# The opening of a one-layer hybrid decoder step: order of the first loads, of the first weight splits, and of the second weight tile's first token group

## What is computed

```python
def rmsnorm(x, g):
    xf = x.astype(jnp.float32)
    y = xf * lax.rsqrt(jnp.mean(xf * xf, axis=-1, keepdims=True) + EPS)
    return (y * g.astype(jnp.float32)).astype(x.dtype)
...
    xn = rmsnorm(h, norm_mix)
    z = xn @ w_in
    conv_out, new_a = causal_dwconv(z[..., O_C:O_H] * z[..., O_H:O_QKV], buf_a, conv_a_w)
    y_a = z[..., O_B:O_C] * conv_out
    qkv, new_qkv = causal_dwconv(z[..., O_QKV:O_G], buf_qkv, conv_qkv_w)
...
    g = -jnp.exp(a_log.astype(f32)) * jax.nn.softplus(z[..., O_A:O_BETA].astype(f32) + dt_bias.astype(f32))
    beta = jax.nn.sigmoid(z[..., O_BETA:IN_W].astype(f32))
```

## Time and profile before

| | us |
|---|---|
| runs of the kernel before, median (lowest to highest of 3) | 1250.08 (1249.86 to 1250.35) |
| the profiled execution, its own time | 1247.68 |
| its span | 1245.9 |
| TensorE busy | 1231.8 (99%) |
| VectorE busy | 789.4 (63%) |
| GpSimd busy | 647.4 (52%) |
| ScalarE busy | 455.5 (37%) |

### The profile page before, as it was taken

One profiled execution on the slowest core, in us unless ns is written; L12 is line 12 of the kernel. 1 busy time (PEld: TensorE's weight loads), 2 busy tenths in 40 slices (PEclk: granted clock), 3 DMA queues, 4 the chain that ended last, 5 costly groups with the idle time before them and its releaser, 6 DMA issues.

```text
span 1245.9 us, 20234 instructions
## 1 busy us (share of the span) xinstructions
PE 1231.8 (99%) x7854; PEld 1083.5 (87%) x7854; DVE 789.4 (63%) x1258; ACT 455.5 (37%) x790; POOL 647.4 (52%) x500
## 2 busy tenths in 40 slices
PE   7999999999999999999999999999999999999998
PEld 6899999899999999998878888888887888877886
DVE  6466899535554655645997686565566667556642
ACT  6465654421212212214333333333434533433412
POOL 2333110112112221214889898888789989787730
PEclk9999999999999999999999999999999999999999
DMA  6122672843223323231145344444655442542012
GB/s 206 45 80 71 173 206 77 216 140 94 78 76 105 92 69 87 78 91 50 48 165 172 124 158 139 140 144 153 227 170 203 166 139 102 187 128 92 18 56 85
DMA packets 163793, 151.05 MB, mean 121 GB/s; under 512 B 21079, under 2 KB 139251, under 8 KB 161010
## 3 DMA queue, kind: packets, MB, share of 16 engines
q1 hardware_dynamic: 140722, 136.88, 34.8%
q10 hardware_dynamic: 22976, 12.88, 3.8%
HBM read 103.25 MB, written 46.49 MB: 120 GB/s over the span
## 4 chain that ended last, share of the span: by engine, by line
PE 95%; issue 1%; DVE 1%; POOL 1%; DMA 1%; ACT 0%; SPq 0%; POOLq 0%; DVEq 0%; ACTq 0%
PE banks L2374 15%; PE banks L2376 15%; PE banks L2377 15%; PE banks L1808 12%; PE banks L1810 11%; PE banks L1809 11%; PE banks L2405 1%; PE banks L2391 1%; PE banks L2503 1%; PE banks L2502 1%; PE banks L2507 1%; PE banks L1994 1%; PE banks L2319 1%; DMA w_raw<-in_w_in 1%; PE banks L1987 1%
## 5 line engine op out<-in xcount | busy, mean ns | idle before, releaser
L1808 PE MATMUL banks<-xn_high,w_high 128*128 128x384 f32 (+1 forms) x672 | 226.9, 338 | 1.0 <-DVE xn_low L2586 0.9
L1810 PE MATMUL banks<-xn_high,w_low 128*128 128x384 f32 (+1 forms) x672 | 219.8, 327 | 0.0
L1809 PE MATMUL banks<-xn_low,w_high 128*128 128x384 f32 (+1 forms) x672 | 219.6, 327 | 0.0
L1027 POOL TENSOR_TENSOR w_low<-w_raw,w_high 128x1024 fp32r<-128x1024 f32 x30 | 77.9, 2598 | 231.2 <-ACT w_high L1297 231.2
L3362 DVE TENSOR_TENSOR hT<-hT,banks 128x512 f32<-128x512 f32 x148 | 98.3, 684 | 97.6 <-PE banks L2377 96.5
L1808 PEld LDWEIGHTS banks<-xn_high,w_high 128*128 128x128 f32 x672 | 127.8, 190 | 5.1 <-issue 1.2
L2374 PE MATMUL banks<-op_high,set_high 128*128 128x512 f32 x336 | 131.8, 392 | 0.0
L2376 PE MATMUL banks<-op_low,set_high 128*128 128x512 f32 x336 | 130.9, 390 | 0.0
L2377 PE MATMUL banks<-op_high,set_low 128*128 128x512 f32 x336 | 130.9, 389 | 0.0
L1809 PEld LDWEIGHTS banks<-xn_low,w_high 128*128 128x128 f32 x672 | 128.1, 191 | 0.0
L1810 PEld LDWEIGHTS banks<-xn_high,w_low 128*128 128x128 f32 x672 | 127.6, 190 | 0.0
(11 more groups left out here) (421 smaller groups left out, 2765.5 us busy)
## 6 DMA issues: line engine op xcount, KB each, us to landing
op_raw<-ops_kept SPq DMA_DIRECT2D x21, 1024.0 KB, 4.9
w_up_raw<-in_w_up SPq DMA_DIRECT2D x16, 1024.0 KB, 6.6
w_raw<-in_w_in SPq DMA_DIRECT2D x28, 512.0 KB, 4.6
ops_kept<-u_rows SPq DMA_DIRECT2D x28, 512.0 KB, 2.7
ops_kept<-u_T SPq DMA_DIRECT2D x42, 256.0 KB, 2.4
w_down_half<-in_w_down SPq DMA_DIRECT2D x3, 2048.0 KB, 9.5
w_down<-in_w_down SPq DMA_DIRECT2D x24, 256.0 KB, 4.0
w_raw<-in_w_out SPq DMA_DIRECT2D x8, 512.0 KB, 4.0
```

The costliest lines, as they stand in the source:

```text
L1027: pool.tensor_tensor(w_l[n % 2][:, :, :], w_raw[n % 2][:, :, :], w_h[n % 2][:, :, :].bitcast(F32), ALU.subtract).then_inc(w_low, 1)
L1808: pe.matmul(bank[:, 0:w], w_h[n % 2][:, k, :], hi[:, c0:c0 + w], start=(k == first), stop=False)
L1809: pe.matmul(bank[:, 0:w], w_h[n % 2][:, k, :], lo[:, c0:c0 + w], start=False, stop=False)
L1810: ins = pe.matmul(bank[:, 0:w], w_l[n % 2][:, k, :], hi[:, c0:c0 + w], start=False, stop=(k == last))
```

## The change

- x_small is loaded on ScalarE's queue behind c_main, ahead of the norm weights; SyncE's queue begins with x_big[0] and holds weight tiles 0 and 1 one behind the other, then x_big[3:5], ab_raw and x_big[5:8].
- The low part of weight tile 0 is made by GpSimd (after the power of token tile 3), that of weight tile 1 by VectorE (after scale_x(3)); the high part of weight tile 1 is made by ScalarE right after the eighth slice's.
- On TensorE, weight tile 0 with group 0 multiplies high weights slice by slice as the slices come, and the low weights from k = 5 on; then weight tile 1 with group 0 follows at once (it was step u = 3, behind the ab products), and the first ab product is made in two halves with turned slices between them.
- Idle products: 6, 2 and 1 of 104 columns ahead of token tiles 0, 1 and 2, where 3 of 208 stood ahead of tile 0.
- The ab products use banks 2, 6 and 7; slices of groups 1 and 2 are turned into four banks (4 to 7), four ahead, where they were five and five; the history rows go to banks 4 and 5.
- ScalarE's squares 4 and 5 follow the high part of weight tile 1, then the ab weights' high part, then square 6; GpSimd makes the ab weights' low part after the power of token tile 5.
- The products finish in another order, so waits on acc_done use in_done(n, g): tile 0's groups finish as 1, 3, 4 and tile 1's as 2, 5, 6. The parts left out of the diff below are this replacement of `3 * n + g + 1` or `3 * (n - 1)` at seven further waits.

```diff
@@ -394,6 +394,12 @@
 
+        def in_done(n, g):
+
+            if n < 2:
+                return ((1, 3, 4), (2, 5, 6))[n][g]
+            return 3 * n + g + 1
+
         def out_bank(n, g):
@@ -606,16 +612,17 @@
 
-        SQUARE_AFTER = {7: (4, 5, 6), 8: (7,), 10: (8,)}
+        SQUARE_AFTER = {7: (4, 5), 8: (7,), 10: (8,)}
         AB_AFTER = 9
-        IDLE_PRODUCTS = (3, 0, 0)
-        TURN_AHEAD = 5
+        IDLE_PRODUCTS = (6, 2, 1)
+        TURN_AHEAD = 4
+        AB_BANKS = (2, 6, 7)
         SEEDED = 1
 
         def turn_bank(g, k):
 
             m = KT * g + k
-            return k if g == 0 else 3 + (m - KT) % 5
+            return k if g == 0 else 4 + (m - KT) % 4
 
@@ -713,8 +720,6 @@
 
-            sp.dma_start(x_small[0:NS, :], xs_v).then_inc(s_xin[0], 16)
-            sp.dma_start(x_small[NS:C0, :], meta_tokens).then_inc(s_xin[0], 16)
             sp.dma_start(x_big[:, 0:1, :], xp_v[:, 0:1, :]).then_inc(s_xin[1], 16)
@@ -848,10 +853,12 @@
                     step(3 * (n - 3) + 1)
-                load(n)
+                if n != 1:
+                    load(n)
                 if n == 0:
+                    load(1)
+                    sp.dma_start(x_big[:, 3:5, :], xp_v[:, 3:5, :]).then_inc(s_xin[4], 16)
                     sp.dma_start(ab_raw[:, :, :], w_in_v[:, :, O_A:O_A + 8]).then_inc(s_ahead, 16)
-                    sp.dma_start(x_big[:, 3:5, :], xp_v[:, 3:5, :]).then_inc(s_xin[4], 16)
                     sp.dma_start(x_big[:, 5:8, :], xp_v[:, 5:8, :]).then_inc(s_xin[5], 16)
@@ -1023,13 +1030,15 @@
                 if n >= 2:
-                    pool.wait_ge(acc_done, 3 * (n - 1))
+                    pool.wait_ge(acc_done, in_done(n - 2, 2))
                 pool.tensor_tensor(w_l[n % 2][:, :, :], w_raw[n % 2][:, :, :], w_h[n % 2][:, :, :].bitcast(F32),
                                    ALU.subtract).then_inc(w_low, 1)
 
             for t in range(NT):
                 x_power(t)
                 if t == 3:
+                    split_low(0)
+                if t == 5:
                     pool.wait_ge(ab_hi, 1)
@@ -1127,7 +1136,7 @@
                     history_a(i)
-                if n not in LOW_BY_DVE:
+                if n and n not in LOW_BY_DVE:
                     split_low(n + 1)
@@ -1287,13 +1296,15 @@
             act.dma_start(cm[:, :], c_main[:, 0:2 * P + 2 * C0 + 2 * NH]).then_inc(s_const, 16)
+            act.dma_start(x_small[0:NS, :], xs_v).then_inc(s_xin[0], 16)
+            act.dma_start(x_small[NS:C0, :], meta_tokens).then_inc(s_xin[0], 16)
             act.dma_start(rows_n[0:8, :], norm_mix.rearrange("l (k p) -> (l k) p", p=P)).then_inc(s_norm, 16)
             act.dma_start(rows_n[8:16, :], norm_ffn.rearrange("l (k p) -> (l k) p", p=P)).then_inc(s_norm, 16)
             def split_high(n):
 
                 act.wait_ge(w_load[n % 2], 16 * (n // 2 + 1))
                 if n >= 2:
-                    act.wait_ge(acc_done, 3 * (n - 1))
+                    act.wait_ge(acc_done, in_done(n - 2, 2))
                 act.activation(w_h[n % 2][:, :, :], w_raw[n % 2][:, :, :], ACT.Copy).then_inc(w_high, 1)
@@ -1308,7 +1319,7 @@
                 act.wait_ge(ab_made, g + 1)
-                act.activation(abT[:, c0:c0 + w], ps[7 - g % 2][0:16, 0:w], ACT.Copy).then_inc(ab_kept, 1)
+                act.activation(abT[:, c0:c0 + w], ps[AB_BANKS[g]][0:16, 0:w], ACT.Copy).then_inc(ab_kept, 1)
 
@@ -1320,14 +1331,17 @@
                                scale=tn[:, k:k + 1]).then_inc(x_high, 1)
-                if m == 3:
+                if m == KT - 1:
+                    act.wait_ge(w_high, 1)
+                    split_high(1)
+                for t in SQUARE_AFTER.get(m, ()):
+                    square_x(t)
+                if m == KT - 1:
                     act.wait_ge(s_ahead, 16)
                     act.activation(ab_w[:, :, 0:8], ab_raw[:, :, :], ACT.Copy).then_inc(ab_hi, 1)
-                for t in SQUARE_AFTER.get(m, ()):
-                    square_x(t)
+                    square_x(6)
                 if m == AB_AFTER:
                     keep_ab(0)
-            split_high(1)
             keep_ab(1)
...
@@ -1824,7 +1838,7 @@
                 c0 = GROUPS[g][0]
-                pe.wait_ge(x_low, m - 4 if m >= KT + 5 else m - KT + 4)
+                pe.wait_ge(x_low, m - 3)
                 for t in GTILES[g]:
@@ -1835,7 +1849,7 @@
                 for _ in range(count):
-                    pe.matmul(ps[7][:, GROUPS[0][1]:], cm[:, 0:P], cm[:, 0:512 - GROUPS[0][1]], start=True, stop=True)
+                    pe.matmul(ps[7][:, GROUPS[0][1]:GROUPS[0][1] + 104], cm[:, 0:P], cm[:, 0:104], start=True, stop=True)
 
@@ -1848,45 +1862,75 @@
 
-            def made_ab(g):
+            def made_ab_high(g):
 
                 w0, w = GROUPS[g]
                 if g == 0:
                     pe.wait_ge(ab_lo, 1)
-                if g == 2:
-                    pe.wait_ge(ab_kept, 1)
                 for k in range(KT):
-                    pe.matmul(ps[7 - g % 2][0:16, 0:w], ab_w[:, k, 0:16], xh[:, k, w0:w0 + w], start=(k == 0), stop=False)
+                    pe.matmul(ps[AB_BANKS[g]][0:16, 0:w], ab_w[:, k, 0:16], xh[:, k, w0:w0 + w], start=(k == 0), stop=False)
+
+            def made_ab_low(g):
+
+                w0, w = GROUPS[g]
                 for k in range(KT):
-                    ins = pe.matmul(ps[7 - g % 2][0:16, 0:w], ab_w[:, k, 0:16], xl[:, k, w0:w0 + w], start=False,
+                    ins = pe.matmul(ps[AB_BANKS[g]][0:16, 0:w], ab_w[:, k, 0:16], xl[:, k, w0:w0 + w], start=False,
                                     stop=(k == KT - 1))
                 ins.then_inc(ab_made, 1)
 
-            pe.wait_ge(w_low, 1)
-            for m in range(KT):
-                pe.wait_ge(x_low, m + 1)
-                dense_part(0, 0, normed, [m])
-            made_ab(0)
-            for m in range(KT, KT + 4):
-                turn_x(m)
+            def small_part(n, weights, part, k, start=False, stop=False):
+
+                w = GROUPS[0][1]
+                ins = pe.matmul(in_bank(n, 0)[:, 0:w], weights[:, k, :], part[:, k, 0:w], start=start, stop=stop)
+                if stop:
+                    ins.then_inc(acc_done, 1)
+
+            pe.wait_ge(w_high, 1)
+            for k in range(KT):
+                pe.wait_ge(x_low, k + 1)
+                small_part(0, w_h[0], xh, k, start=(k == 0))
+                small_part(0, w_h[0], xl, k)
+                if k == 5:
+                    pe.wait_ge(w_low, 1)
+                    small_part(0, w_l[0], xh, 0)
+                if k >= 5:
+                    small_part(0, w_l[0], xh, 2 * k - 9)
+                    small_part(0, w_l[0], xh, 2 * k - 8)
+            small_part(0, w_l[0], xh, KT - 1, stop=True)
+
+            pe.wait_ge(w_high, 2)
+            for k in range(KT):
+                small_part(1, w_h[1], xh, k, start=(k == 0))
+                small_part(1, w_h[1], xl, k)
+            pe.wait_ge(w_low, 2)
+            for k in range(KT):
+                small_part(1, w_l[1], xh, k, stop=(k == KT - 1))
+
+            made_ab_high(0)
+            turn_x(KT)
+            turn_x(KT + 1)
+            made_ab_low(0)
+            turn_x(KT + 2)
+            turn_x(KT + 3)
             for m in range(KT, 3 * KT):
                 pe.wait_ge(x_low, m + 1)
+                if m == 2 * KT:
+                    pe.wait_ge(ab_kept, 1)
                 dense_part(0, m // KT, normed, [m % KT])
-                if m == KT:
-                    pe.wait_ge(ab_kept, 1)
-                    turn_x(m + 4)
                 if m + TURN_AHEAD < 3 * KT:
                     turn_x(m + TURN_AHEAD)
 
             pe.wait_ge(s_row, 112)
             for f in range(QKVW // P):
-                ins = pe.transpose(ps[3][:, 28 * f:28 * f + 28], rows_q[:, P * f:P * f + P], eye[0:28, 0:28])
+                ins = pe.transpose(ps[4][:, 28 * f:28 * f + 28], rows_q[:, P * f:P * f + P], eye[0:28, 0:28])
             for f in range(CONV // P):
-                ins = pe.transpose(ps[4][:, 19 * f:19 * f + 19], rows_a[:, P * f:P * f + P], eye[0:19, 0:19])
+                ins = pe.transpose(ps[5][:, 19 * f:19 * f + 19], rows_a[:, P * f:P * f + P], eye[0:19, 0:19])
             ins.then_inc(rows_turned, 1)
 
-            made_ab(1)
-            made_ab(2)
+            made_ab_high(1)
+            made_ab_low(1)
+            made_ab_high(2)
+            made_ab_low(2)
 
@@ -1899,6 +1943,7 @@
                 pe.wait_ge(ab_kept, 3)
+                pe.wait_ge(rows_kept, 3)
                 for t in range(NT):
@@ -2245,11 +2290,10 @@
                             pe.wait_ge(w_low, n + 1)
-                        if u == 3:
-                            pe.wait_ge(rows_kept, 3)
                         if u >= 4:
                             acc_free(pe, (u - 4) // 3, (u - 4) % 3)
-                        dense_part(n, g, normed, range(KT))
+                        if u != 3:
+                            dense_part(n, g, normed, range(KT))
```

(17 more changed lines are left out.)

## The result

| | kernel before | changed kernel |
|---|---|---|
| median of 17 runs each (lowest to highest) | 1247.93 us (1244.49 to 1251.1) | 1251.64 us (1250.21 to 1256.08) |
| ratio, 95% interval | | 1.0035 (1.0024 to 1.0046) |
| profiled execution, span | 1247.68, 1245.9 | 1255.94, 1254.1 |

The change makes the kernel slower by 0.35%, about 4.4 us; 1248.6, which is 1.5 us faster, was forecast.

A forecast was written before the change was run, and what follows sets the result against it. TensorE bounds the kernel, at work 1231.8 of 1245.9 us. Gain 3.1 minus stall 1.6 makes 1.5: 1247.68 to 1246.2, plus 2.40 for the median, 1248.6; forecast's own range 1247.8 to 1249.6, whole range 1246.6 to 1251.4.

The forecast's parts named there:

- the loads: Opening: x_small behind c_main on ScalarE's queue, first square at 5.2 instead of 4.58, all at nothing under ScalarE's other work.
- The case chosen: Opening: clock up before the dense products, which start at 12.3 instead of 13.50; chance 0.44, 1248.6 us.
- rival B: Opening: clock low until about 17, dense at 13.5, steady at 30.4, 0.5 us slower, 1250.6; chance 0.20.
- The stall: TensorE behind the last ab products, waiting for ScalarE to evict tile 0's group 0: a new 1.6 us.
- The chain from slice 8 to steady work: Group 1's opening: from ScalarE's high part of slice 8 to steady TensorE work, 7.12 us as before.
- E: Behind the new stall: TensorE's wait brings the clock down, costing another 1.7 us, 1250.3; chance 0.11.
- D's low stretch: Behind the tiny ab transposes: the low clock at 58.1 would be gone too, 1.7 us more, 1246.9; chance 0.17.
- From S to M: S: start of the first dense product, forecast 12.3; M: start of the first tiny ab transpose, forecast 53.4.
- C: Opening: GpSimd's split holds up VectorE's xn_low, dense starts 2.2 to 2.9 later, 1251.3 taken; chance 0.08.

The follow-up runs named there:

- Number 4: Changed kernel, same order on ScalarE's queue, SyncE's big token tiles held back until x_small has landed; 1248.55 us, one profiled run.
- number 1: Changed kernel with x_small back at the head of SyncE's queue, all else as changed; 1246.6 us, ratio 1.0010.
- number 9: Changed kernel, x_small first on SyncE's queue, tile 0's evictions early, idle products ahead of token tile 0 alone, second time; 1245.69 us, ratio 0.9998.
- Numbers 8 to 10: Changed kernel, x_small first on SyncE's queue, early evictions; 8 and 9: idle products ahead of token tile 0 alone, 0.9993 and 0.9998; 10: none, 0.9996.
- number 2: Kernel before with one edit: x_small loaded on ScalarE's queue behind c_main; 1249.61 us, ratio 1.0032.
- numbers 7 to 10: 7: changed kernel, x_small first on SyncE's queue, tile 0's evictions ahead of keep_ab(1); 1246.12 us, ratio 1.0004. Others: see Numbers 8 to 10.
- numbers 1 and 5 to 10: 5: changed kernel without idle products ahead of token tiles 1 and 2, 1249.54 us; 6: changed kernel, tile 0's evictions ahead of keep_ab(1), 1249.55 us.

## Why the prediction was wrong, step by step

**The step that failed is the first: the loads.** I put the small tile's landing at 5.2, "between 4.58 and about 5.5", with 0.4 for one issue more and half a microsecond for "the shared engines"; it was 8.47. The move did two things that I priced as one: it put 192 KB behind 180 KB, and it let three half-megabyte tiles into the other queue beside them, with nothing small ahead. Number 4 separates them: on the same queue, without the tiles, each load needs at most 2.8 us, and the first square starts at 4.34. The step cost 3.96 us (number 1 against the changed kernel), and no range of mine held it: added to 1248.6 it gives 1252.6, beyond 1251.4.

**The case chosen was the wrong one.** The forecast had the clock up from about 10. In the changed kernel, all 16 transposes of tiles 1 and 2 still run at 0.24 each, and the idle products took 2.82 + 0.97 + 0.38 (from start to start), not 2.45 + 0.8 + 0.2. Number 1 has the loads nearly as I assumed them (TensorE begins at 5.41; I had 5.7), and its dense products begin at 14.24, not 12.3: of these 1.9 us, 1.5 are the transposes of the two tiles (1.71 + 1.75, not 0.9 + 1.05), the rest are idle products.

Nearest came rival B, the clock low until about 17: dense at 13.5, the first group done at 18.5, steady at 30.4, 0.5 us lost. Number 1 shows 14.24, 18.40 and 30.51, M 0.74 later and a ratio of 1.0010. That B's chain meets it within 0.1 us is luck, for two errors cancel. Its start was too early: by its own terms tile 2's transposes fill TensorE from 12.35 to 14.2. And its first group was too long, 5.0 us at half rate: here the clock was up at 14.85, and the group took 4.16, paced by VectorE. B had 0.20 of the chance and the forecast 0.44.

**What was right.** The stall: 1.6 forecast; M - S falls by 1.6 without it. The chain from slice 8 to steady work: 7.12. E: the granted clock did not fall behind the stall in any of the profiles. D's low stretch behind the tiny transposes is there again in the changed kernel's profile and in those of numbers 4 and 9, and absent in the other eight: it comes and goes with the execution. From S to M the forecast had 53.4 - 12.3 = 41.1; measured 41.4 in every changed version with the stall, 39.7 to 39.8 in every one without, whether the first dense products ran slow or fast.

C, VectorE held by GpSimd's split, did not come, but the changed kernel hardly tests it, for its split is over at 17.65 and xn_low begins at 17.50. Numbers 8 to 10 do test it; number 9, POOL and DVE:

```profile
11.81 2.38 POOL L1036 TENSOR_TENSOR w_low<-w_raw,w_high 128x1024 fp32r<-128x1024 f32 x1
12.26 3.63 DVE L2628 SCALAR_TENSOR_TENSOR xn_low<-banks,tn,xn_high 128x304 fp32r<-128x304 f32 x8 [0.53 <-ACT xn_high L1332]
```

The split runs to 14.19, the eight xn_low take 3.63, as without it. So the Trainium skill's sentence on two SBUF inputs (GPSIMD Engine Reference, Key points) had it.

**Where the expected gain went.** The constancy from S to M explains it. In the changed order the first group is paced by VectorE's 0.45 per slice, so slow products cost it nothing. In the kernel before TensorE paces it: from S to the first ab product it is 5.10 with fourteen slow products (profiled) but 3.94 with three or four (number 2), and from there to M 36.3 in both. So M - S is 41.37 or 40.23, and by an estimate some 39.7 with no slow product (the slow stretch of number 2 is 1.1 us, half of it lost). The overlap does work, but it gains only against an execution of before that had met a late clock. The one that I had to reckon with was such a one. Against one with the clock up, the new order gains nothing from S to M even without its stall (39.8), and loses 1.6 with it. That the single profiles vary so agrees with the Trainium skill (TensorE: Matmul & The Clock Gate, Part 1), which says that the point of the rise wanders from run to run.

The timed runs carry no rows, but each has its mean granted clock. It is 0.996 or 0.997 in the five profiles with a low stretch behind the opening, and 0.999 or 1.000 in the seven without. Take the runs from 0.999 up, on the chip of numbers 7 to 10. Numbers 8 to 10 have a median of 1243.8 (11 runs), the kernel before 1245.1 (30 runs): 1.3 us, not 2.0 to 2.5. If a version's M in the timed runs is that of its profile, M of before is about 54 in them; numbers 1 and 5 to 10, each worked out so against the kernel before on its chip, give 53.7 to 54.5. That lies between the profiled 54.87 and the 53.2 of an early clock (13.50 + 39.7). The rest is the low stretch: 23 of the 34 runs of numbers 8 to 10 are below 0.999, but 14 of the 44 of the kernel before, and such runs are about 2 us longer (medians 1245.7 and 1247.2). Why they are more frequent there stays open. All this is worked out from the runs, not shown by an experiment, and the dividing line was drawn after the runs.

## What to carry to other kernels

A small load that starts the first chain belongs at the head of a queue, ahead of every big transfer on any queue; moving it to a free queue does not protect it, it takes turns there. Before a wait is priced from the profiled execution, ask whether it is paced by something that differs between executions, such as the clock: a gain against the slow case is not a gain against the median. And where a block of work is pulled forward, look for what it had covered: here 1.6 us of eviction, which cost one loop on ScalarE to win back.

## What was not expected of the hardware

In the changed kernel's profile a VectorE operation with both inputs in SBUF (usual 1.22 to 1.41 us) took 6.17, while GpSimd ran operations of 1.3 us one behind the other, undisturbed. Timeline, DVE and POOL:

```profile
624.61 6.17 DVE L3362 SCALAR_TENSOR_TENSOR u_rows<-u_rows,h_squares 128x1024 f32<-128x1024 f32 x1
```

```profile
624.67 1.31 POOL L1172 TENSOR_TENSOR w_up_sum<-w_up_raw 128x512 f32<-128x512 f32 x1
625.90 1.32 POOL L1184 TENSOR_TENSOR set_low<-w_up_sum,set_high 128x512 fp32r<-128x512 f32 x1
627.16 1.31 POOL L1166 TENSOR_TENSOR w_up_sum<-w_up_sum,w_up_raw 128x512 f32<-128x512 f32 x1
628.40 1.28 POOL L1184 TENSOR_TENSOR set_low<-w_up_sum,set_high 128x512 fp32r<-128x512 f32 x1
```

GpSimd's row ended at 629.68 and the operation at 630.78, 1.1 us later, nearly its usual time: as if it had begun only when GpSimd paused. Number 2 shows the same (625.55 and 626.63). TensorE waited 3.0 us for the operation right behind it, and directly after that hole the granted clock was low (columns as in the earlier trace rows):

```profile
632.60:636.00 3.40, 3.40 (x13) 2.19 (x14) 2.77 (x3) 1.51 (x2) 3.40 (x3) 0.50 0.49 186
```

The last but two number, 0.50, is the granted clock. From M to the end the spans tell the price: 1189.3 to 1189.4 us in seven of the twelve profiles; 1190.9 to 1191.0 in the three with one low stretch behind the tiny transposes (before, numbers 4 and 9); 1194.5 in the changed kernel's, which has that stretch as well, and 1193.1 in that of number 2, where the same operation took 6.17 too and has its low stretch behind it. So this event costs 3.5 to 3.7 us, nearly as much as the whole effect under study; in the other ten profiles the longest such operation is 2.43. Whether the late opening makes it likelier stays open: two of the five profiles with late loads show it, and none of the seven others.
